# Delta rule: the transposed neighbours of the first doubling level taken by an identity product on TensorE, not by VectorE transpositions

## The reference, cut to what matters

```
a_mat = where(strict_lower, (k * beta) @ k.T * gamma, 0)   # per chunk and head
t_mat = a_mat + eye
u = solve(t_mat, v * beta);  w = solve(t_mat, k * beta * exp(gc))
# over the chunks, with the state S:
v_new = u - w @ S
o     = (q * exp(gc)) @ S + (q k.T * gamma) @ v_new
S     = S * exp(gc_last) + (k * exp(gc_last - gc)).T @ v_new
```

## Time and profile before

| | |
|---|---|
| Median of 3 runs | 3741.86 us |
| The profiled execution, own time | 3742.21 us |
| Its span, first to last instruction | 3740.3 us |
| Outside the span | 1.9 us |
| Mean granted TensorE clock | 0.994 |
| Busy: TensorE, VectorE, ScalarE, GpSimd | 98%, 57%, 42%, 2% of the span |
| Instructions | 50657 |
| The woven stage | about 379 to 711 us |

### The profile page before, as it was taken

How to read it: one execution, slowest core, us unless ns; L and a number is a source line. 1 busy time by engine, 2 the same in 40 slices (tenths; PEclk the granted TensorE clock), 3 DMA queues, 4 the chain that set the end, 5 groups by cost and what they waited for, 6 DMA issues and landing times.

```text
span 3740.3 us, 50657 instructions
## 1 busy us (share of the span) xinstructions
PE 3668.1 (98%) x21121; PEld 2968.0 (79%) x21121; DVE 2148.3 (57%) x3262; ACT 1580.2 (42%) x2544; POOL 81.5 (2%) x85
## 2 busy tenths in 40 slices
PE   8999888899999999999999999999999999999998
PEld 5887677778888878888788889888787788788887
DVE  5641677775345578757588564366655266555333
ACT  5451666634333444435353452333443333434333
POOL 0000121000000000000000000000000000000000
PEclk9999999999999999999999999999999999999999
DMA  5124321324322222222222222222222222223222
GB/s 197 46 74 107 83 59 39 116 91 108 110 92 95 96 80 80 91 95 94 87 80 91 96 91 87 89 85 85 82 93 94 93 85 81 83 92 117 96 96 85
DMA packets 118490, 340.27 MB, mean 91 GB/s; under 512 B 20072, under 2 KB 31864, under 8 KB 118136
## 3 DMA queue, kind: packets, MB, share of 16 engines
q1 hardware_dynamic: 116024, 331.52, 26.1%
q0 software_dynamic: 2240, 5.51, 0.7%
HBM read 318.47 MB, written 20.06 MB: 91 GB/s over the span
## 4 chain that ended last, share of the span: by engine, by line
PE 94%; DVE 3%; ACT 2%; issue 1%; DMA 0%; SPq 0%; ACTq 0%; DVEq 0%
PE ps L329 54%; PE ps L307 28%; PE ps L1324 1%; PE ps L808 1%; PE ps L2815 1%; PE ps L1032 1%; PE ps L1675 1%; PE ps L1642 1%; DVE n_s L1764 1%; PE ps L1335 1%; DVE g_D L1508 0%; PE ps L2250 0%; PE ps L2277 0%; ACT n_s L1709 0%; PE ps L2239 0%
## 5 line engine op out<-in xcount | busy, mean ns | idle before, releaser
L329 PE MATMUL ps<-a,w_hi 128*128 128x512 f32 (+1 forms) x6064 | 1838.0, 388 | 2.5 <-ACT l_vf L2657 0.8
L329 PEld LDWEIGHTS ps<-a,w_hi 128*128 128x128 f32 x6064 | 1110.0, 188 | 260.5 <-issue 10.6
L329 PE MATMUL ps<-a,w_lo 128*128 128x512 f32 (+1 forms) x3032 | 1147.3, 385 | 0.0
L268 DVE TENSOR_TENSOR w_lo<-w_raw,w_hi 128x1024 fp32r<-128x1024 f32 x539 | 658.0, 1221 | 397.8 <-ACT w_hi L263 395.1
L263 ACT ACTIVATE w_hi<-w_raw 128x1024 fp32r<-128x1024 f32 x539 | 563.6, 1050 | 516.7 <-DMA w_raw<-in_w_mlp 323.9
L329 PEld LDWEIGHTS ps<-a,w_lo 128*128 128x128 f32 x3032 | 562.5, 188 | 119.7
L307 PE MATMUL ps<-h_hi,w_hi 128*128 128x512 f32 x1528 | 485.4, 399 | 0.0
L307 PE MATMUL ps<-h_hi,w_lo 128*128 128x512 f32 x1528 | 479.1, 395 | 0.0
L307 PE MATMUL ps<-h_lo,w_hi 128*128 128x512 f32 x1528 | 478.8, 395 | 0.0
L374 DVE TENSOR_TENSOR h_lo<-u_sq,h_hi 128x512 fp32r<-128x512 f32 x192 | 132.9, 692 | 461.4 <-ACT h_hi L364 460.5
L390 DVE TENSOR_TENSOR xT<-xT,ps 128x1024 f32<-128x1024 f32 x191 | 232.9, 1219 | 247.3 <-PE ps L307 246.4
(11 more groups left out here) (392 smaller groups left out, 2962.0 us busy)
## 6 DMA issues: line engine op xcount, KB each, us to landing
w_raw<-in_w_mlp SPq DMA_DIRECT2D x384, 512.0 KB, 3.4
w_raw<-in_w_in SPq DMA_DIRECT2D x107, 512.0 KB, 3.4
w_raw<-in_w_out SPq DMA_DIRECT2D x48, 512.0 KB, 3.4
n_bias<-na_tab SPq DMA_DIRECT2D x36, 256.0 KB, 4.7
xT<-in_x SPq DMA_DIRECT2D x8, 512.0 KB, 8.5
x<-xT SPq DMA_DIRECT2D x2, 2048.0 KB, 8.3
g_row<-gate_rows SPq DMA_DIRECT2D x16, 256.0 KB, 3.3
xT<-x SPq DMA_DIRECT2D x2, 2048.0 KB, 11.8
```

Source lines behind the costliest of these rows:

```text
L268: nc.vector.tensor_tensor(w_lo[u.z][:, :], w_raw[u.z][:, :], w_hi[u.z][:, :].bitcast(F32), ALU.subtract).then_inc(w_split[u.z], 1)
L329: last = nc.tensor.matmul(ps[:, bank, 0:t1 - t0], w[:, k * P:(k + 1) * P], a[:, h, low, k, t0:t1], start=(i_k == 0 and i == 0), stop=(i_k ...
```

## The change

The four VectorE transpositions per step (two per direction) go. In their place `pairs_pe` issues for each direction 8 small products on TensorE: for each head and each half of the partitions, the 64x64 diagonal block of g_A is the stationary operand, and every second column of the identity `fold` is the moving one, so that the transposed elements arrive in PSUM bank 2 of the direction, behind `keys_keys` in the same bank. All is fp32, which takes two instructions per product. The masked product on VectorE then reads PSUM and not g_D. The semaphore AT, which VectorE raised for itself, is now raised by TensorE.

`pairs_pe` waits for g_A. In step n it stands on TensorE after `step_out(m, 0)` for direction 0 and after `step_out(m, 1)` for direction 1, ahead of the state update. For step 0 it stands after the seventh block of the last projection unit, and after the eighth.

```diff
--- before.py
+++ after.py
@@ -815,7 +815,11 @@
                 if end and at == 5:
                     pe.wait_ge(nv_act, NV_LAST.index(gbank(1, 2)) + 1)
                     keys_keys(pe, 0, 1)
+                if end and at == 6:
+                    pairs_pe(pe, 0, 0)
             last.then_inc(mm_done[u.z], 1)
+            if end:
+                pairs_pe(pe, 0, 1)
 
         def nv1_act(act):
             for at, b in enumerate(NV_LAST):
@@ -1273,18 +1277,23 @@
             dve.wait_ge(gs["dec"], once(n, d))
             nc.vector.tensor_tensor(g_A[d][:, :, :], pbank(gbank(d, 2)), (g_dec if n else g_dec0)[d][:, :, :], ALU.mult).then_inc(gs["A"], 1)
 
+        def pairs_pe(pe, n, d):
+
+            pe.wait_ge(gs["A"], once(n, d))
+            for h in range(GH):
+                for i in range(2):
+                    part = side(i)
+                    last = nc.tensor.matmul(halves(stacked(gbank(d, 2)), 0, 1 - d)[part, h], g_A[d][part, h, part],
+                                            halves(const("fold").unsqueeze(1), 0, 1 - d)[part, 0], start=True, stop=True)
+            last.then_inc(gs["AT"], 1)
+
         def identity_act(act, d):
             nc.scalar.activation(g_Dc[d][:, :, :], const("fold").unsqueeze(1).to_broadcast([P, GH, GRID]), ACT.Copy).then_inc(gs["ident"], 1)
 
         def first_level(dve, n, d):
 
-            dve.wait_ge(gs["A"], once(n, d))
-            for i in range(2):
-                ins = nc.vector.transpose(g_D[d][side(i), :, :], g_A[d][side(i), :, side(i)])
-            ins.then_inc(gs["AT"], 1)
-            yield
             dve.wait_ge(gs["AT"], once(n, d))
-            nc.vector.tensor_tensor(halves(g_gu[d][:, :, :], 0, 1 - d), halves(g_D[d][:, :, :], 0, 1 - d), lev_mask(0, d), ALU.mult)\
+            nc.vector.tensor_tensor(halves(g_gu[d][:, :, :], 0, 1 - d), halves(stacked(gbank(d, 2)), 0, 1 - d), lev_mask(0, d), ALU.mult)\
                 .then_inc(gs["lev"], 1)
             yield
             dve.wait_ge(gs["ident"], once(n, d))
@@ -1378,7 +1387,9 @@
                     pe.wait_ge(nv_act, TC)
                 if s == 0 and 0 < n < TC:
                     step_out(m, 0)
+                    pairs_pe(pe, n, 0)
                     step_out(m, 1)
+                    pairs_pe(pe, n, 1)
                     for d in range(2):
                         pe.wait_ge(gs["kd"], once(m, d))
                         heads(gbank(d, 0), g_kd[d], g_vn[d]).then_inc(gs["su"], 1)
```

## The result

The changed kernel takes 3755.11 us in the median of 7 runs (3752.78 to 3758.97), the one before 3743.08 in 7 runs beside them (3740.86 to 3745.55). The ratio is 1.0033, 95% interval 1.0023 to 1.0043: 12.0 us slower, where 10.2 were forecast. The profiled executions, 3755.11 and 3742.21 us, have spans of 3753.2 and 3740.3, 12.9 us apart.

A forecast was written before the change was run, and what follows sets the result against it. TensorE, busy 10.00 of 10.00 us at the change of step, was taken as the bound, with VectorE's removed work off the path. 5.7 + 2.0 + 0.5 + 2.0 = +10.2 us gave a forecast of 3752.1 us, range 3743 to 3760.

The forecast's parts named there:

- The four changes to steps 2 to 5: Changes of step where TensorE is always busy: two calls less 0.1 us hidden, 1.42 us each, +5.7 us.
- The price of a call: Each call of 8 products on TensorE: 0.67 us for eight rounds plus 0.09 for going to small tiles, 0.76 us.
- Steps 6 and 7: First call partly fills TensorE's wait for n_z, costing 0.23 us, the second 0.76: about 1.0 each, +2.0 us.
- Step 1: First call hidden in a 0.98 us gap, second delays L1701 by 0.76; VectorE's removed transpositions help there: +0.5 us.
- Step 0: At the last projection unit, direction 1's g_A and the memsets come later, the first L1764 at 382.8: +2.0 us.
- scatter around the forecast: Clock falls in the stage, one more or fewer within range; rival of two fewer gives 3745 us, chance 0.09.
- Cheap calls: Rival: a call's two instructions start together on TensorE, 0.43 us a call, +5.4 us, 3747.3; chance 0.14.
- taking turns: Rival: row tiles of one PSUM bank take turns, 1.43 us a call, +21.2 us, about 3763; chance 0.08.
- The rival that VectorE was the path: At the changes of step, VectorE's freed 1.81 us shorten each: 8 x 1.5 = 12 us less, 3730; chance 0.07.

The follow-up runs named there:

- Products twice: The changed kernel with each call's 8 products issued twice, 16 in a row: 3764.41 us, ratio 1.0060 against the kernel before.
- step 0 on VectorE: The changed kernel with step 0's first level transposed by VectorE as before: 3753.24 us, ratio 1.0031 against the kernel before.
- the products alone: The kernel before, keeping its VectorE transpositions, with the added products of steps 1 to 7 issued beside them and read by nobody: 3750.91 us, ratio 1.0026.
- tiles of 32: The changed kernel with its products cut to 32x32 tiles, 32 instructions on four tiles per call: 3751.07 us, ratio 1.0024 against the kernel before.
- kernel before with both moves: The kernel before with the state update behind L1701 and the outputs' eviction behind level 1's mask: 3734.43 us, ratio 0.9982; once more, 3735.51.

## Why the prediction was right

**The four changes to steps 2 to 5, forecast +5.7 us.** Measured on the change stretch: +1.40 to +1.45 each, together 5.7. The price of a call was right too: 0.58 us in the chain and 0.2 more for the first matmul pair behind it (0.42 for 0.22), 0.78 where 0.76 was taken. Products twice shows that its two parts were right, 0.47 and 0.3. Their place was not quite: the prediction had 0.67 for the rounds and 0.09 for going over, where 0.2 us of the call fall on the first 128x128 matmul pair behind it.

**Steps 6 and 7, +2.0.** Measured +0.96 each, 1.9. The first call went into the wait for n_z, as the timeline of the change to step 6 shows: the call at 633.12, `step_out(m, 1)` at 633.71. Its gap was 0.53 and is gone.

```profile
633.12 0.66 PE L1286 MATMUL ps<-consts,g_A 64*64 64x32 f32 x16
...
633.71 0.49 PE L1376 MATMUL ps<-g_qd,g_S 128*128 128x128 f32 x2
```

**Step 1, +0.5.** The change stretch is 0.78 longer (0.76 forecast for L1701), the rest of the step 0.18 shorter, +0.60. The first call (425.37) is hidden ahead of the second `step_out`, the mask waits 0.91, and L1344 starts 2.58 us behind L1764, where it was 3.40: the transpositions are out of the way, as forecast, and ScalarE's L1728 at 433.40 takes over.

```profile
425.37 0.65 PE L1286 MATMUL ps<-consts,g_A 64*64 64x32 f32 x16
...
426.25 1.13 PE L1377 MATMUL ps<-g_qk,g_vn 128*128 128x128 f32 x8 [0.23 <-DVE n_z L1802]
...
427.31 0.66 PE L1286 MATMUL ps<-consts,g_A 64*64 64x32 f32 x16
...
428.02 0.29 DVE L1296 TENSOR_TENSOR g_gu<-ps,g_lev 128x128 f32<-128x128 f32 x1 [0.91 <-PE ps L1286]
...
430.21 0.47 ACT L1764 ACTIVATE n_of<-ps,params 128x256 f32<-128x256 f32 x1 [1.83 <-PE ps L1712]
...
432.79 0.67 PE L1344 MATMUL ps<-g_gu,g_D 64*64 64x32 f32 x32
...
433.40 1.06 ACT L1728 ACTIVATE n_pt<-ps 128x512 f32<-128x512 f32 x2
```

**Step 0, +2.0.** The first L1775 came 1.93 us later, counted from the first exponentials (L1300, at 332.14 before and 333.16 after). The mechanism is the one forecast: VectorE stands 4.97 us for the first call, so that g_A of direction 1 comes late (379.75), TensorE's weight loads of the second call wait 0.37 us for it, and the memsets end where the attention should begin.

```profile
378.44 0.66 PE L1286 MATMUL ps<-consts,g_A 64*64 64x32 f32 x16
...
379.15 0.29 DVE L1296 TENSOR_TENSOR g_gu<-ps,g_lev 128x128 f32<-128x128 f32 x1 [4.97 <-PE ps L1286]
...
379.75 0.69 DVE L1278 TENSOR_TENSOR g_A<-ps,g_dec 128x512 f32<-128x512 f32 x1
...
380.62 0.65 PE L1286 MATMUL ps<-consts,g_A 64*64 64x32 f32 x16
...
382.13 0.27 DVE L1493 MEMSET g_Dt<- 64x256 f32 x1
...
383.77 0.62 DVE L1775 CUSTOM_DVE_ANT_0 n_s<-ps,n_bias 128x512 f32<-128x512 f32 x1
```

Not all of it reached the end. By the exponentials of step 1 the changed profile was only 1.06 us behind, counted in the same way, and its second profile 0.23 ahead; the profile with step 0 on VectorE was 0.63 behind. The clock is at half speed for 14 to 21 us just there in all of them, and it comes back at different moments. Over all fourteen profiles of this document step 0, from its exponentials to those of step 1, lasted 84.8 to 86.8 us in the eight without products there and 85.8 to 87.5 in the six with them, 86.3 and 86.7 in the mean. So the sum's +2.0 is right where it was read, at the first L1775, but it was carried on in full without a reason, and only about half a microsecond of it is seen a step later. What step 0 costs in the end stays open between 0 and 2 us.

**What was not in the sum.** The steps' rests, outside the change stretches, came to -0.2, -0.3, +0.4, -1.8, 0.0, +1.7 and +2.6 us for steps 1 to 7, +2.4 in all. The profile before starts the stage's first exponentials 1.0 us earlier, which belongs to the projections. So the 12.9 us of the two spans are 1.0 ahead of the stage, 1.1 from step 0, 8.4 from the changes of step, 2.4 from the rests. The 8.4 were forecast as 8.2, and that is what the mechanism earns. That the whole, 10.2, came so near 12.0 is in part luck: step 0 gave 0.9 less than its term, and the 1.0 and the 2.4 stand in no term. The rests go with the clock. Step 4's 1.8 is the fall at 559 to 567 us, which the changed kernel doesn't have. Step 6's 1.7 may well not belong to the change: the kernel without transpositions, with the old change stretches, took 36.94 there too, and the one with the products alone 34.2, less than before. Step 7's 2.6 comes with a second fall, and it came in each of the six profiles with products and TensorE's old order (44.0 to 44.2 us outside the change stretch) and in neither of the two without them (41.4 in both). So the clock was not only a scatter around the forecast, as the prediction had it, but here also a cost of some 2 us that came again. It can be the difference between 10.2 and 12.0, as far as the interval (8.6 to 16.1 us) allows to speak of one; no run set it apart.

**The rivals.** Cheap calls and taking turns are both out by the call's 0.58 us, and the second also by the products issued twice. The Trainium skill's rule on row tiles in one PSUM bank ("TensorEngine Tiling (Array Packing)", Gotcha 1: PSUM Pressure) does not describe this. Two row tiles wrote to different partitions of one bank, and in the trace of a call the instructions of the two tiles start 7 ns apart, pair after pair, every 58 ns; L1335, with four tiles over two banks, has the same 58 ns a round. With tiles of 32, four row tiles wrote to one bank at 32 ns a round. What no run did is send the two halves of a product into different banks. The rival that VectorE was the path is out for the kernel as it was, and half true of the kernel with the state update moved, which the prediction did not foresee as a condition: TensorE's free time was not what it needed, but a ScalarE that no longer comes last. Even there the freed time paid only a part of the price (the change stretch is 1.3 us longer, the rest of an undisturbed step 0.65 shorter), and with the eviction moved as well it paid nothing in an undisturbed step.

## What to carry to other kernels

Before moving work from one engine to another, ask of the place, not of the span: the engine with 98% was the one without a free microsecond at the place, and 14 us taken off the other engine were worth nothing. A small product among full-size ones costs its rounds and 0.3 us for the way in and out, so by this sum few long bursts beat many short ones. And what an order of work leaves idle can be worth as much as the exchange costs: one block of 16 matmul instructions issued behind two others, which ScalarE waited for, and one eviction moved gave 8 us, where the exchange cost 12.

## What the runs showed of the hardware

- On 64x64 tiles a round of weight load and matmul with 32 columns takes 58 ns, whether two tiles work (L1286 in the changed kernel) or four (L1335 before); with 64 columns on two tiles (L1347) it takes 58 ns too. On 32x32 tiles with 16 columns it takes 32 ns; four tiles then start an instruction every 8 ns or so (32 in 0.26 us).
- VectorE's masked product took 291 ns from SBUF and from PSUM alike.
- The granted clock falls to its lower level (1.2 GHz for 2.4) after TensorE has stood idle for part of the attention's waits, and comes back while it is busy. When it fell at 559.2 us in the kernel before, TensorE's matmuls had waited 0.75 us for L1764 and stood in a wait of 0.91 us for L1517; from 563 to 567 us, where it came back (at 566.1), TensorE was busy for 4.00 of 4.00 us.
- In two kernels that were profiled twice, the falls of steps 6 and 7 came in the same steps again (619.5 and 618.3, 643.4 and 642.2, 667.3 and 666.1, 691.2 and 690.0 us in the changed kernel). The kernel before with both moves, whose undisturbed steps are 1.8 us shorter than those of before, has them elsewhere. But the length of a step alone does not fix them: without any transposition the steps are as long as before, and the falls at 559 and 614 us are gone, with others at 601 and 635. In the kernel before with both moves 4 to 5 of the 12.6 us that its undisturbed steps had gained are missing from the median; that the clock took them is likely, but was not isolated.
